# Column groups of 512, 512 and 64 tokens in the output projections and feed-forwards of a hybrid decoder step

## What is computed

```
mix = concat(mixer outputs) @ w_out          # 1024 -> 1024
y = y + mix
y = y + swiglu(rmsnorm(y, norm_ffn), ffn_gate, ffn_up, ffn_down)
# swiglu: (silu(h @ gate) * (h @ up)) @ down, 1024 -> 2816 -> 1024
```

## Time and profile before

| | us |
|---|---|
| median of three runs | 3757.83 |
| lowest and highest of the runs | 3752.47, 3758.24 |
| span of the profiled execution | 3747.8 |
| PE busy, of the span | 3449.9 (92%) |
| PE weight loads busy | 2863.5 (76%) |
| DVE busy | 1465.7 (39%) |
| ACT busy | 830.8 (22%) |
| POOL busy | 560.4 (15%) |

### The profile page before, as it was taken

How to read it: one execution, slowest core, us unless ns; L and a number is a source line. 1 busy time by engine, 2 the same in 40 slices (tenths; PEclk the granted TensorE clock), 3 DMA queues, 4 the chain that set the end, 5 groups by cost and what they waited for, 6 DMA issues and landing times. The chain is left out here.

```text
span 3747.8 us, 62202 instructions
## 1 busy us (share of the span) xinstructions
PE 3449.9 (92%) x25987; PEld 2863.5 (76%) x25987; DVE 1465.7 (39%) x2698; ACT 830.8 (22%) x1576; POOL 560.4 (15%) x384
## 2 busy tenths in 40 slices
PE   8888887898778779999999999999989999999996
PEld 5566666554456569999999995656649999999996
DVE  4465566422566653323232224232323322222321
ACT  2332222111456422111111112222213211111110
POOL 0000000204000014222222221000003321222221
PEclk9899999999799979999999999999999999999998
DMA  2000000303200131111111102011122111111112
GB/s 102 21 19 13 20 14 8 133 23 84 69 1 1 64 110 53 52 32 52 37 51 34 45 28 113 23 70 47 42 101 104 52 51 34 49 39 40 51 34 103
DMA packets 73473, 189.20 MB, mean 50 GB/s; under 512 B 26916, under 2 KB 41188, under 8 KB 70132
## 3 DMA queue, kind: packets, MB, share of 16 engines
q1 hardware_dynamic: 59956, 156.92, 12.3%
q0 software_dynamic: 8960, 28.32, 2.3%
q10 hardware_dynamic: 4352, 1.05, 0.1%
HBM read 161.34 MB, written 29.04 MB: 51 GB/s over the span
## 5 line engine op out<-in xcount | busy, mean ns | idle before, releaser
L177 PE MATMUL ps<-ff_x,ff_wh 128*128 128x384 f32 (+1 forms) x3960 | 774.9, 328 | 0.0
L177 PEld LDWEIGHTS ps<-ff_x,ff_wh 128*128 128x128 f32 x3960 | 668.7, 188 | 0.8
L177 PE MATMUL ps<-ff_x,ff_wl 128*128 128x384 f32 (+1 forms) x2112 | 465.5, 328 | 0.0
L177 PEld LDWEIGHTS ps<-ff_x,ff_wl 128*128 128x128 f32 x2112 | 360.7, 188 | 0.0
L520 DVE TENSOR_TENSOR resid<-resid,ps 128x384 f32 (+1 forms) x240 | 113.2, 527 | 386.8 <-PE ps L177 386.8
L2549 PE MATMUL ps<-act,gl_w 128*128 128x384 f32 (+1 forms) x768 | 244.2, 473 | 0.0
L177 PE MATMUL ps<-ff_hh,ff_dh 128*128 128x384 f32 (+1 forms) x1056 | 233.4, 329 | 7.2 <-DVE ff_hl L512 4.6
L177 PE MATMUL ps<-ff_hh,ff_dl 128*128 128x384 f32 (+1 forms) x1056 | 232.7, 328 | 0.0
L177 PE MATMUL ps<-ff_hl,ff_dh 128*128 128x384 f32 (+1 forms) x1056 | 232.7, 328 | 0.0
L2549 PEld LDWEIGHTS ps<-act,gl_w 128*128 128x128 f32 x768 | 144.1, 192 | 90.1 <-issue 10.4
L507 DVE TENSOR_TENSOR ff_prod<-ff_silu,ps 128x384 f32<-128x384 f32 x132 | 62.3, 527 | 349.6 <-PE ps L177 349.6
(11 more groups left out here) (607 smaller groups left out, 5405.3 us busy)
## 6 DMA issues: line engine op xcount, KB each, us to landing
ff_w<-in_wg SPq DMA_DIRECT2D x44, 512.0 KB, 3.5
ff_w<-in_wu SPq DMA_DIRECT2D x44, 512.0 KB, 3.5
ff_wd<-in_wd POOLq DMA_DIRECT2D x48, 256.0 KB, 3.0
ff_wd<-in_wd POOLq DMA_DIRECT2D x32, 320.0 KB, 3.3
rw_w<-in_w_rwkv SPq DMA_DIRECT2D x14, 512.0 KB, 3.5
ns_past<-in_cache_slc SPq DMA_DIRECT2D x48, 128.0 KB, 2.2
np_w<-in_w_nsa SPq DMA_DIRECT2D x8, 652.0 KB, 8.2
resid<-in_x SPq DMA_DIRECT2D x1, 4352.0 KB
```

The costliest lines, as they stand in the source:

```text
L177: mm = pe.matmul(g.ps[:, bank + c, 0:n], w[:, k, :], x[:, o:o + n], start=(first and i == 0), stop=(last and i == 2))
```

## The change

A second table of column groups, FCH, is added, and the output projections and feed-forwards use it wherever they used CH. The loads of the inputs and the mixers keep CH.

```diff
 CH = ((0, 384), (384, 384), (768, 320))
+FCH = ((0, 512), (512, 512), (1024, 64))
...
     for i, (w, x) in enumerate(passes):
-        for c, (o, n) in enumerate(CH):
+        for c, (o, n) in enumerate(FCH):
             mm = pe.matmul(g.ps[:, bank + c, 0:n], w[:, k, :], x[:, o:o + n],
                            start=(first and i == 0), stop=(last and i == 2))
...
             def sums(c):
-                o, n = CH[c]
+                o, n = FCH[c]
                 pe.matmul(g.ps[:, 6 + c % 2, 0:n], g.mean[:, :], sqsum[:, o:o + n], start=True, stop=True).then_inc(norm.mean_ready.sem, 1)
...
             def root(c):
-                o, n = CH[c]
+                o, n = FCH[c]
                 act.wait_ge(norm.mean_ready.sem, 3 * g.norms + c + 1)
...
                 dve.wait_ge(so.done, T0 + t + 1)
-                for c, (o, n) in enumerate(CH):
+                for c, (o, n) in enumerate(FCH):
                     m = dve.tensor_tensor(g.resid[:, t, o:o + n], g.resid[:, t, o:o + n], g.ps[:, 3 * (t % 2) + c, 0:n], ALU.add)
...
-            for c, (o, n) in enumerate(CH):
+            for c, (o, n) in enumerate(FCH):
                 dve.wait_ge(norm.root_ready.sem, 3 * g.norms + c + 1)
                 dve.reciprocal(rs[:, o:o + n], rs[:, o:o + n])
...
-                    for c, (o, n) in enumerate(CH):
+                    for c, (o, n) in enumerate(FCH):
                         m = dve.tensor_tensor(silu[:, o:o + n], rs[:, o:o + n], g.ps[:, c, 0:n], ALU.mult)
...
-                    for c, (o, n) in enumerate(CH):
+                    for c, (o, n) in enumerate(FCH):
                         m = dve.tensor_tensor(prod[:, o:o + n], silu[:, o:o + n], g.ps[:, 3 + c, 0:n], ALU.mult)
...
-                        for c, (o, n) in enumerate(CH):
+                        for c, (o, n) in enumerate(FCH):
                             r = flat(g.resid[:, ds(2 * i + t, 1), o:o + n])
                             m = dve.tensor_tensor(r, r, g.ps[:, 3 * t + c, 0:n], ALU.add)
```

## The result

The changed kernel takes 4011.45 us (median of four runs, 4005.85 to 4016.94), the kernel before 3755.62 us in the same comparison. The ratio is **1.0684**, 95% interval 1.0668 to 1.07. The forecast was 3993 us and a range of 3885 to 4065: slower, as forecast, and 18 us beyond the middle. (The profiled execution took 4007.45 us by itself, 1.6 us over its span. The 10.0 us between median and span of the kernel before are therefore not time around the instructions, as was said ahead of the prediction: most of them are the difference between one execution and another. Since they were carried over unchanged, they moved nothing.)

What follows compares the result with a forecast made beforehand. TensorE's matmuls on line 177 were taken to bound 1793 of 3748 us. Passes +238 us, waits -4.0, norm +0.2, half clock +0.7 gave +235 on 3757.8: 3993 us, range 3885 to 4065.

Steps and rivals of the forecast that it cites:

- The number of matmuls and where they bound: Line 177: the same 10656 matmuls before and after, in two stretches of about 1010 us each after the change.
- The short group: Group of 64 columns in each pass: 109 ns to the next matmul, held by the weight load; bounds 107 and 123.
- The long groups: The two groups of 512 in each pass: 2 x 228.9 = 457.8 ns with 15.6 ns loss each; lower end 430.6.
- The waits of PE: PE's waits for DVE and POOL shrink as PE gets slower: -2.4 us for DVE, -1.6 us for POOL.
- DVE's shapes: DVE's empties: 695 ns for 512 columns, 191 for 64, sum of three 1.58 us before and after; costed at nothing.
- The half-clock pass: Some 8 passes at the two starts: 1067 ns instead of 907, load at twice its 107 ns; +0.7 us.
- the distance of starts after 64 columns: Line 177, short windows of the profile after: 0.11 us forecast; under 0.05 would prove the load hidden and the forecast wrong.
- The constant loss: Line 177 at full clock: each float32r matmul loses 15.6 ns beyond its columns, whatever its size.
- No change: Rival on line 177: next load stays hidden, a pass is 500 ns in either split, 3758 us; chance 4%.
- faster: Rival after the short matmul: two loads held in reserve, a pass of 487 ns, -46 us, 3712 us; chance 3%.
- Twice the load: Rival at the group of 64: two loads, 214 ns, a pass of 672 ns, +611 us, 4366 us; chance 5%.
- The loss is gone: Rival on line 177: load is the floor but long matmuls absorb the 15.6 ns; pass 538 ns, 3890 us; chance 28%.

## Why the prediction was right, step by step

**The number of matmuls and where they bound.** Right: 10656 matmuls, two stretches that hold the whole 258 us. They are 1025 us each, where "about 1010" was written.

**The short group.** Forecast 109 ns, between 107 and 123. The place is 108.4. The mechanism (a short matmul can't hide the load behind it, and the load goes by weight columns) is shown by the same 108 ns at 64, 128 and 192 token columns, by the doubled short matmul, and by the weights of 64 columns, which brought the place to 55.0.

**The long groups: the term that was mis-sized.** Forecast 228.9 ns each, between 215.3 and 228.9. The places are 235.7 and 229.8, so both lie above the bounds. The loss was taken as the mean of the kernel before, 15.6 ns, and used as the upper bound too; at 512 columns it is 22.4 ns in the group behind the short one and 16.5 in the next. A pass was forecast at 567 and is 574 ns. The two long groups are 7.7 ns above their 457.8 together, and the short one is 0.6 below its 109. Over 3552 passes that 7 ns is 25 us, against the 23 by which the growth of the span (258) exceeds the forecast (235).

**The small terms.** The waits of PE, after, in the first stage and then in the second:

```profile
PE ps L178 <- DVE ff_hl L513: 0.9, 2, 0.5
```

```profile
PE ps L178 <- DVE ff_hl L513: 0.9, 2, 0.5
```

That is 1.8 us in place of twice the 2.3 of the earlier trace rows, and the wait for POOL's `ff_dl` is not among PE's waits: 2.8 and 2.6 us gained where 2.4 and 1.6 were forecast. This is most of the 2 us between 25 and 23. DVE's shapes, to be set beside the earlier trace rows:

```profile
L521 DVE TENSOR_TENSOR resid<-resid,ps 128x512 f32 x160 | 102.9, 684 | 458.5 <-PE ps L178 458.5
...
L521 DVE TENSOR_TENSOR resid<-resid,ps 128x64 f32 x80 | 17.1, 214 | 0.0
```

2 x 684 + 214 = 1582 ns, as forecast, though the ends were 695 and 191. DVE's idle time grew by 72 us, 19%. The half-clock pass was forecast at 1067 ns; four of them start at

```profile
1367.82 1.28 PE L178 MATMUL ps<-ff_mix_high,ff_wh 128*128 128x512 f32 x3 [7.24 <-POOL ff_wl L243]
1368.91 1.26 PE L178 MATMUL ps<-ff_mix_high,ff_wl 128*128 128x512 f32 x3
1369.97 1.25 PE L178 MATMUL ps<-ff_mix_low,ff_wh 128*128 128x512 f32 x3
1371.04 1.20 PE L178 MATMUL ps<-ff_mix_high,ff_wh 128*128 128x512 f32 x2
```

1.09 us apart at the start, then 1.06 and 1.07. By the starts of the loads the places are 430, 427 and 210 ns, so the estimate of a load at twice its 107 ns was right to 4 ns.

**A sign that was wrong.** The prediction named the distance of starts after 64 columns as the test: 0.11 us right, under 0.05 wrong. It reads 0.03 (from 2000.11 to 2000.14), and the load isn't hidden. The test should have been on the starts of the loads, or on whole passes. The rows of before had the warning: to read the earlier trace rows the prediction itself had to take off a first load, 0.11 us, that lies inside the first record.

**The constant loss.** "I read it as a constant for each matmul" was good to some nanoseconds only. With all loads hidden a pass loses 40 ns beyond its 453.3 at 384, 352 and 352, 43 at 368, 368 and 352, 44 at 512, 288 and 288, 47 at 384, 384 and 320, and 52 at 416, 416 and 256. Place by place the table gives more: the place less the columns at 2.4 GHz is 11 ns for the group of 256 (117.4 - 106.7) and 24 for the 416 right behind it (196.9 - 173.3). Behind a group of 256 columns or fewer a long one loses more than the next of its size: 235.7 and 229.8, 221.9 and 216.4, 196.9 and 191.5. Why is not shown.

**The rivals.** No change and faster are out with 1.0684. Twice the load is out: 5328 loads a stretch. "The loss is gone" (538 ns a pass) had 28%, more than it deserved. Its support, a smaller loss after 384 columns than after 320, was one printed digit; to the nanosecond it is real but small (14.0 and 15.5 against 17.4 ns), and it doesn't go on: at 512 columns the loss is 16 to 22 ns.

## What to carry to other kernels

Where each matmul loads its own weights, a matmul is worth the larger of its columns (and its loss) and its load. A load of 128 float32r weight columns takes 108 ns at full clock in these runs, and hides behind 256 token columns (117 ns) but not behind 192; the limit is near 235 columns, an estimate: at 2.4 GHz the 9 ns between 117.4 and 108.4 are some 22 columns under 256. So leave no group short: 512, 512 and 64, in both orders tried, is the worst of the splits, and every split with no group under 256 was within 0.6% of the kernel before. Three groups are the fewest that the banks allow here; more were not tried. A record that starts early is no proof of work: go by the starts of the loads, or count whole passes.

## What the runs showed of the hardware that was not expected

- A matmul's record can begin before its own weights are in: 0.03 us after the short one, with about 0.08 us of waiting inside it (a record of 0.48 us where the median is 0.39, and 0.11 us to the next load).
- A load is made for every float32r matmul, even where the weights are those of the matmul before (ratio 1.0678 with the short group in the middle).
- The time between two loads that nothing hides follows the weights' width and the clock: 108.4 ns for 128 columns, 55.0 for 64, and 210 for 128 at half clock.
- The loss of a float32r matmul at full clock, 11 to 24 ns by place, hangs on the group sizes and their order by a rule that these runs don't show. Halving the width of the weights took about 3 ns off. In the kernel before at half clock it is not there. What it is stays open; splits of four matmuls, or one size in every group, were not tried. At 384, 352 and 352 it costs least, 0.5% of the kernel under the split before.
